# Attention stage of a two-block model kernel: projections by seven half-size products per 256 tokens, three weight slots, weight sums in the fourth slot, outputs kept in memory

## The reference, cut to what matters

```python
p  = h  @ w_in                      # 256 x 2048 times 2048 x (q | gate | z | k | v | xbc | dt)
pc = hc @ w_in[:, base:]            # the context tokens need k, v, xbc, dt of the first block
q, k, kc = rms_norm(heads(q)), rms_norm(heads(k)), rms_norm(heads(kc))
ya = neighbourhood_attention(q, k, v, kc, vc, rpb)      # softmax over 256 latent and 256 context keys
ya = ya * silu(gate)
yb = ...                                                # state space part, from z, xbc, dt
out = concatenate([ya, yb]) @ w_out
```

## Time and profile before

| | us |
|---|---|
| median of 3 runs | 2831.66 (2830.11 to 2832.17) |
| the profiled execution, its own time | 2830.7 |
| its span, first to last instruction | 2828.5 |
| TensorE busy in it | 2776.7 (98%) |
| VectorE busy | 1314.0 (46%) |
| ScalarE busy | 441.6 (16%) |
| GpSimd busy | 51.4 (2%) |
| mean granted TensorE clock | 0.992 of full |

### The profile page before, as it was taken

How to read it: one execution, slowest core, us unless ns; L and a number is a source line. 1 busy time by engine, 2 the same in 40 slices (tenths; PEclk the granted TensorE clock), 3 DMA queues, 4 the chain that set the end, 5 groups by cost and what they waited for, 6 DMA issues and landing times. The chain is left out here.

```text
span 2828.5 us, 38622 instructions
## 1 busy us (share of the span) xinstructions
PE 2776.7 (98%) x15840; PEld 2235.0 (79%) x15840; DVE 1314.0 (46%) x2317; ACT 441.6 (16%) x867; POOL 51.4 (2%) x72
## 2 busy tenths in 40 slices
PE   7999999999999999999999999999999999999999
PEld 1467866776686566666668888999999899999999
DVE  3643343333243245555555003665666665555543
ACT  0221111111111122222222001111111111121211
POOL 0010000000000000000000000000000000000000
PEclk9999999999999999999999999999999999999999
DMA  9874555655464133333332544555554545545542
GB/s 384 306 248 154 178 170 171 200 181 160 154 202 130 40 105 105 104 104 104 104 104 95 187 150 151 176 166 164 176 169 158 178 134 145 147 150 158 160 139 86
DMA packets 379174, 445.20 MB, mean 157 GB/s; under 512 B 20308, under 2 KB 351560, under 8 KB 378312
## 3 DMA queue, kind: packets, MB, share of 16 engines
q1 hardware_dynamic: 351088, 352.76, 40.6%
q0 software_dynamic: 19520, 75.50, 7.7%
q10 hardware_dynamic: 8472, 15.58, 1.5%
HBM read 439.56 MB, written 4.26 MB: 157 GB/s over the span
## 5 line engine op out<-in xcount | busy, mean ns | idle before, releaser
L529 PE MATMUL bank<-hT,w 128*128 128x128 f32 (+2 forms) x6128 | 1263.4, 365 | 6.1 <-ACT hT L1154 4.6
L529 PEld LDWEIGHTS bank<-hT,w 128*128 128x128 f32 x6128 | 898.2, 193 | 329.8 <-issue 296.1
L529 PE MATMUL bank<-w,hT 128*128 128x256 f32 (+2 forms) x2048 | 394.0, 353 | 0.0
L529 PEld LDWEIGHTS bank<-w,hT 128*128 128x128 f32 x2048 | 350.1, 190 | 48.9 <-issue 10.0
L1154 ACT ACTIVATE work<-bank 128x512 f32<-128x512 f32 (+3 forms) x282 | 146.1, 539 | 1300.3 <-PE bank L529 1295.1
L529 PE MATMUL bank<-yT,w 128*128 128x256 f32 (+1 forms) x1888 | 343.2, 342 | 1.4 <-DVE yT L1870 1.0
L529 PEld LDWEIGHTS bank<-yT,w 128*128 128x128 f32 x1888 | 307.3, 191 | 33.0 <-DVE yT L1870 1.2
L529 PE MATMUL bank<-hT,work 128*128 128x128 f32 x2352 | 279.5, 275 | 0.0
L529 PEld LDWEIGHTS bank<-hT,work 128*128 128x128 f32 x2352 | 270.9, 192 | 0.0
L1701 DVE SCALAR_TENSOR_TENSOR work<-xT,silc,work 128x512 f32<-128x512 f32 x240 | 180.5, 752 | 43.2 <-DMA xT<-in_ada_w 35.2
L1154 ACT ACTIVATE work<-work 128x512 f32<-128x512 f32 (+4 forms) x267 | 150.1, 562 | 245.2 <-DVE work L1767 149.4
(11 more groups left out here) (172 smaller groups left out, 1831.8 us busy)
## 6 DMA issues: line engine op xcount, KB each, us to landing
w<-in_na_ssd_w_in SPq DMA_DIRECT2D x48, 2048.0 KB, 8.4
xT<-in_ada_w POOLq DMA_DIRECT2D x64, 1024.0 KB, 5.6
w<-in_sc_w_in SPq DMA_DIRECT2D x32, 2048.0 KB, 10.3
w<-in_w_in SPq DMA_DIRECT2D x32, 2048.0 KB, 10.4
w<-in_na_ssd_w_out SPq DMA_DIRECT2D x16, 2048.0 KB, 8.4
w<-in_ada_w SPq DMA_DIRECT2D x12, 2048.0 KB, 11.2
w<-in_na_ssd_w_in SPq DMA_DIRECT2D x16, 1024.0 KB, 7.3
w<-in_sc_w_out SPq DMA_DIRECT2D x8, 2048.0 KB, 8.2
```

Source lines behind the costliest of these rows:

```text
L529: return nc.tensor.matmul(dst, lhsT, rhs, start=start, stop=stop, skip_group_check=free)
```

## The change

In `na` the tiles of all iterations are numbered n = 4i, 4i+1, ... (q, gate, k, v). A unit is one tile with 256 tokens: q, gate, k latent, k context, v latent, v context, six per iteration. The very first unit stays as it was; the other 47 are made by seven products of half size (7 x 8 matmuls of 128 columns, `na_unit`). Tiles go round three slots (n mod 3). The fourth slot now holds the weight sums (`turn`, four places of 8 x 128, three per tile in rotation); the fourth sum overwrites a quarter of the tile. VectorE makes them in two halves (`sums_one`, `sums_two`), one tile ahead. Sums of the latent tokens lie in the first half of `yT`, those of the context tokens in the second. So the attention outputs no longer fit there: `na_out` writes them to `yout`, ScalarE's queue stores them to memory after each pair of heads (`na_store`), and SyncE loads all of them back in the first `ssd` iteration. ScalarE copies the products to `staged0`, VectorE combines them (`na_combine`), and squares and the sigmoid start from the combined values. The loops of `na` are written out for all eight iterations. Norm and shift of the context tokens come after the first unit. The stage after changes only in its semaphore counts.

```diff
+    def na_places(n):
+        return [turn[:, (3 * n + m) % 4, :, :] for m in range(3)]
...
-        gp.wait_ge(norm_mul, 2 * DC)
+        gp.wait_ge(norm_mul, DC)
         iterations(gp, 8, late_chunks)
...
+                if phase == "ssd":
+                    return sp.wait_ge(acc_full, na_filled((30, 31, 29)[s]))
...
-        iterations(sp, 8, na)
+        for n in range(32):
+            if n < 3:
+                sp.wait_ge(ada_used, 10 + n)
+            else:
+                sp.wait_ge(acc_full, na_filled(n - 3))
+            at = (COL_Q, COL_GATE, COL_K, COL_V)[n % 4] + (n // 4) * TILE
+            load(na_slot(n), w_in[:, :, at:at + TILE])
+            if n % 4 == 1 and n > 4:
+                na_biases(n // 4 - 1)
...
                 sp.dma_start(xT[:, :, :].rearrange("p a b -> p (a b)"), x_scratch).then_inc(x_back, 16)
+                sp.wait_ge(y_saved, 16 * 8)
+                sp.dma_start(yT[:, 0:DC, :].rearrange("p a b -> p (a b)"), y_scratch).then_inc(y_back, 16)
...
+        def na_unit(i, u, midway=None):
...
+            wait(pe, acc_free, k - 1)
+            if n == 0:
+                featured(bank[0][:, 0:T], s, 0, T, lambda kc: kc + 1).then_inc(acc_full, 1)
+                featured(bank[1][:, 0:T], s, 1, T).then_inc(acc_full, 1)
+                return
...
+            product(a(0), quarter(s, 0, 0), x(0, 0), None, turned)
+            product(a(1), quarter(s, 1, 0), x(0, 1), None, turned)
...
+            pe.wait_ge(na_t, 3 * n - 2)
+            product(a(2), t1, sums[1], None, turned)
+            pe.wait_ge(na_t, 3 * n - 1)
+            product(a(3), t2, sums[2], None, turned).then_inc(acc_full, 1)
+            if midway:
+                midway()
+            pe.wait_ge(acc_free, k)
+            product(b(0), quarter(s, 0, 1), sums[3], None, turned)
+            product(b(1), quarter(s, 1, 1), sums[4], None, turned)
+            pe.wait_ge(na_t, 3 * n)
+            product(b(2), t4, x(1, 1), None, turned).then_inc(acc_full, 1)
...
+        def na_staging(i, u, part):
...
+            if part == 0:
+                wait(act, n_made, 6 * i + u)
+            width = 2 * P if i + u == 0 else (4 - part) * P
+            A(flat[:, 4 * P * part:4 * P * part + width], bank[part][:, 0:width], ACT.Copy).then_inc(acc_free, 1)
...
+        def na_store(a):
+            act.wait_ge(na_y, 2 * a + 2)
+            act.dma_start(y_scratch[:, 2 * a * T:(2 * a + 2) * T], yout.rearrange("p a b -> p (a b)")).then_inc(y_saved, 16)
...
+        def sums_one(n):
...
+            dve.wait_ge(w_loaded[s], 16 * (EARLY + n // 3 + 1))
+            if n > 1:
+                dve.wait_ge(acc_full, na_filled(n - 2))
+            link(v.tensor_tensor(places[0], quarter(s, 0, 1), quarter(s, 0, 0), ALU.subtract))
+            v.tensor_tensor(quarter(s, 0, 1), quarter(s, 1, 1), quarter(s, 0, 1), ALU.subtract).then_inc(na_t, 1)
+
+        def sums_two(n):
...
+            dve.wait_ge(acc_full, na_filled(n - 1, False))
+            v.tensor_tensor(places[1], quarter(s, 1, 1), places[0], ALU.subtract).then_inc(na_t, 1)
+            dve.wait_ge(na_t, 3 * n - 1)
+            v.tensor_tensor(places[2], quarter(s, 1, 0), places[1], ALU.subtract).then_inc(na_t, 1)
...
+        def na(i):
+            first = is_first(i)
             a = i - 1
-            if not is_first(i):
+            n = 4 * i
...
                 na_biases(a)
                 late_mod(a)
...
+                sums_one(n + 1)
+                late_part(i, 0)
+                sums_two(n + 1)
+                na_combine(i, 0, qraw)
+            sums_one(n + 2)
+            if not first:
                 na_softmax(a, 0, link)
+            sums_two(n + 2)
...
+            na_combine(i, 1, graw)
...
                 na_turned(a, 0)
                 na_softmax(a, 1, link)
...
+            sums_one(n + 3)
...
+            late_part(i, 1)
+            na_combine(i, 2, kraw[:, :, 0:T])
+            if not first:
                 na_out(a, 0)
                 na_turned(a, 1)
+            late_part(i, 2)
+            sums_two(n + 3)
+            late_part(i, 3)
+            na_combine(i, 3, kraw[:, :, T:T + TC])
+            if not first:
                 na_out(a, 1)
+            if i < 7:
+                sums_one(n + 4)
+            late_part(i, 4)
+            late_part(i, 5)
+            na_combine(i, 4, vtok[:, 0:2, :])
             dve.wait_ge(na_ge, i + 1)
...
+            late_part(i, 6)
+            late_part(i, 7)
+            if i < 7:
+                sums_two(n + 4)
...
+            na_combine(i, 5, vtok[:, 2:4, :])
```

More of the change, by code:

```diff
@@ L663, in na @@
             a = i - 1
[L664 to L668 removed]
+            na_unit(i, 0)
             if not first:
                 na_scores(a, 0)
[L671 to L675 removed]
+            na_unit(i, 1)
             if not first:
@@ L889, in _ @@
         norm_halves(1)
-        def product(dst, weights, tokens, ready=None, turned=False, chunks=range(EIGHT)):
-            for kc in chunks:
-                if ready:
-                    pe.wait_ge(ready[0], ready[1] + kc + 1)
-                a, b = weights[:, kc, :], tokens[:, kc, :]
-                last = mm(dst, b if turned else a, a if turned else b, kc == 0, kc == EIGHT - 1)
-            return last
         def banks_free(phase, s, i):
@@ L1208, in _, with shifted @@
         act.wait_ge(mod_ready, 1)
-        for k in range(2):
+        def shifted(k):
             for kc in range(DC):
@@ L1244, in na @@
             if not first:
                 na_exp(a, 0)
[L1246 to L1254 removed]
+            na_staging(i, 1, 0)
@@ L1255, in na @@
+            na_staging(i, 1, 1)
+            na_rms(i, 0)
             if not first:
                 na_exp(a, 1)
-            na_rms(i, 0)
+            for u in (2, 3):
+                na_staging(i, u, 0)
+                na_staging(i, u, 1)
             for ch in range(2):
-                full("na", 2 + ch, i)
-                A(kraw[:, ch, :], bank[ch][:, :], ACT.Copy)
-                A(ksq[:, ch, :], bank[ch][:, :], ACT.Square).then_inc(acc_free, 1)
-            for half in range(2):
-                na_rms(i, 1 + half)
-                full("na", 4 + half, i)
-                wait(act, na_po, 2 * i)
-                A(vtok[:, 2 * half:2 * half + 2, :].rearrange("p a b -> p (a b)"), bank[half][:, :],
-                  ACT.Copy).then_inc(acc_free, 1)
@@ L1269, in _ @@
-        iterations(act, 8, na)
+                na_square(i, 1 + ch, ksq[:, ch, :], kraw[:, ch, :], 3)
+            if not first:
+                na_store(a)
+            na_sigmoid(i)
+            na_staging(i, 4, 0)
+            na_staging(i, 4, 1)
+            na_rms(i, 1)
+            na_staging(i, 5, 0)
+            na_rms(i, 2)
+            na_staging(i, 5, 1)
+        for i in range(8):
+            na(i)
         for h in range(2):
             na_exp(7, h)
+        na_store(7)
         def ssd_setup():
@@ L1675, in na_out @@
             dve.wait_ge(na_po, 2 * a + h + 1)
-            v.tensor_tensor(chunk(yT, 2 * a + h), bank[5][:, 0:T], gsil[:, h, :], ALU.mult).then_inc(na_y, 1)
+            if h == 0:
+                wait(dve, y_saved, 16 * a)
+            v.tensor_tensor(yout[:, h, :], bank[5][:, 0:T], gsil[:, h, :], ALU.mult).then_inc(na_y, 1)
         def silu(out_, raw, sigmoid):
```

269 lines of the change are left out of this document (155 added, 114 removed).

## The result

The changed kernel takes **2819.2 us** (median of 7 runs, 2809.75 to 2821.61); the kernel before took 2830.67 on the same chip (median of 7, 2829.79 to 2835.14). The ratio is 0.995 with a 95% interval of 0.9936 to 0.9964: faster, but by 0.5% where 1.6% was forecast, and outside the range of 2770 to 2802. Every ratio in this document is to the kernel before, timed on the same chip as the kernel it is given for. The profiled execution took 2821.06 us, 37.3 more than the 2783.8 that the sum gave for it.

What follows compares the result with a forecast made beforehand. TensorE, busy 98% of the span, was taken to bound the kernel. 2830.7 - 60.9 (TensorE's work) + 12 (tail stall) + 2 (slower clock) = 2783.8; the median lies 1.0 higher, 2784.8 us, range 2770 to 2802.

Steps and rivals of the forecast that it cites:

- TensorE's work, 60.9 us: Attention stage: units of 12.507 us save 54.5 us in seven iterations and 6.4 in the first, if nothing makes TensorE wait.
- the first rival: Tail: the bias rows land before they are wanted, so no stall; 2770.8 us, chance 0.07.
- The last rival: Attention units: weight loads take turns with matmuls, 0.111 us more per record, 526 us slower, 3358 us; chance 0.01.
- VectorE's work: Attention iteration: weight sums add 19.6 us and combines 11.0, making 66.3 of 89.7 us; total and order fit.
- the schedule: One attention iteration, t = 0 at its first unit: VectorE's results dated against TensorE's needs, `late_sums` ending at 89.7 us.
- GpSimd's chunks: Attention loop: a chunk takes 5.5 us from issue until VectorE goes on; the closest is issued at 71, wanted at 80.
- the smallest reserve: End of an attention iteration: eighth late chunk taken at 83, `late_sums` at 88.0, 5 us to spare.
- small waits in every iteration: Rival, attention loop: late chunks cost 1 to 3 us in each of seven iterations; 2792 to 2806 us, chance 0.15.
- what would show the forecast wrong: Signs: period over 92 us, idle time before `late_sums` or a unit's third product, or a tail still 22 us.
- The tail: After the eighth attention iteration: late bias rows stall TensorE 12 us (9.3 to 18.4), slower clock adds 2 (0 to 4).
- From the first `ssd` product to the end: Everything after the attention tail: the same length as before the change.
- the bound: Rival, attention loop: VectorE limits it through late chunks; gain used up at 12 us late, 2848 us at 14; chance 0.04.

Runs made afterwards that it cites:

- Experiment 5: Changed kernel with the loop's bias rows issued behind the q load, the tail's issued earlier and masked before VectorE's last combine: 2770.6 us, ratio 0.9784.
- experiment 10: Changed kernel, bias transfers of iterations 1 to 6 replaced by aligned 256-byte rows 512 bytes apart, the same six for all partitions: 2796.81 us.
- experiment 7: Changed kernel, bias transfers of iterations 1 to 6 replaced by aligned 256-byte rows spread over a weight matrix: 2800.15 us; the profiled execution took 2812.06.
- experiment 6: Changed kernel, bias transfers of iterations 1 to 6 replaced by the same bytes in 1536-byte rows of a weight matrix: 2799.31 us.

## Why the prediction was wrong

**TensorE's work, 60.9 us: right.** A unit takes 12.5 us and the period, where nothing waits, is 89.77 us (89.7 forecast). Experiment 5 has neither loss, and its span is 2768.0 against 2828.5: 60.5 us less. The sum of the first rival, 2770.8 without a stalled tail, agrees with its 2770.6 to a microsecond. The rule cited from the Trainium skill, TensorE: Matmul & The Clock Gate, section The mechanism, by which, as the prediction reads it, loads and matmuls of whole arrays take turns, does not hold here. A record of 256 columns took 0.216 us in the kernel before (13.82 us for 64) and one of 128 columns 0.1117 (12.507 for 112), so only 0.007 us of a record does not grow with its columns. A load in turn would have to fit into that. The last rival's 0.111 us of load was busy time that runs beside the products.

**VectorE's work: right in size, wrong in the dates of the last chunks.** It is busy 66.46 us in the iteration from 411.9 to 501.8 (66.3 forecast), and its queue kept the dates of the schedule but for chunks seven and eight. **The step that failed** is "GpSimd's chunks: issue at 297.11, VectorE free to go on at 302.64, 5.5 us, and the closest one is issued at 71 and wanted at 80". The two dates came true: the seventh chunk of the second iteration was issued at t = 71 and wanted at 80, counted from 224.48. The landing did not: 16.9 us in place of 5.5. 5.5 us was read from one chunk that met no bias rows; in the same trace of the kernel before, between 200 and 890 us, chunks took 5.3 to 10.4 us. Even by 5.5 this chunk had 3.5 us to spare, not the 5 that the prediction calls the smallest reserve. In the new order the gate load goes out at t = 63 and the bias rows from 63 to 71, and the last three chunks at 63, 71 and 77: SyncE's loads were costed for their own dates only, and the bias rows of the loop were not in the schedule at all. The prediction named the effect as a rival, "small waits in every iteration" (2792 to 2806, chance 0.15), and priced it by idle time alone. Idle was 11.7 us, the slow clock behind it 13.8; with some 1.3 us of smaller pieces that makes 26.8 (22.7 in the periods, 4.1 in the first iteration, which took 85.48 us from its first product to `late_sums` against 81.39 in experiment 5). The period of over 92 us and the idle time before `late_sums` were both on the list of what would show the forecast wrong.

**The tail: right mechanism, size too small.** The stall is 18.69 us against 12, just outside the bounds of 9.3 and 18.4. From the v tile's last product at 873.00: the wait 0.2, the two loads 2.8 (2.3 forecast), the last bias issue 5.3 in (3.7), its landing 11.1 (6.4), the mask 0.96. The term that was mis-sized is the landing, taken from the median of the earlier trace rows, which also have one of 12.9: 4.7 of the 6.7 us. The issues add 1.6 and the loads 0.5. What differs from the kernel before is what comes right behind: 2 MB at 882.00 and 2 MB at 882.74, where SyncE issued nothing more for over 26 us then. The first three of the four bias transfers landed in 8.6, 6.3 and 7.0 us, and the last, issued just before those loads, in 11.1. That the loads make the last landing long was not tried. The sentence of the Trainium skill on DMA: Bandwidth & Descriptors, section Queues, rings and completion order, leaned to the upper half of the bounds. The trace agrees in that direction (18.69), without showing that ring order is the cause. The clock behind it cost 2.8 us (26.2 us of tail without the pause, 23.4 in experiment 5), 2 forecast. In the first 11.5 us behind the pause the granted clock was 0.65.

**From the first `ssd` product to the end**: 1901.0 us against 1898.2, where the same length was forecast. A wait of 0.68 us for `in_ssd_d` and 64 records that took 22.50 instead of 20.80 us make up most of it; the prediction had no term for either.

The whole: 26.8 in the loop, 7.3 in the tail, 2.8 behind it, 36.9 of the 37.3 us missed.

**The rivals that were wrong**: VectorE never became the bound. The one mechanism named there, a chunk that is late by over 5 us, was the right place, but the lateness that it needed (12 us) was not reached: VectorE's longest wait for a chunk was 8.2 us.

## What to carry to other kernels

When work moves to another time in a periodic schedule, list every transfer of every queue that is now in flight together, small ones too, and don't price a landing by a row in which the engines were free. Give a wait on TensorE's path its idle time and something for the slower clock behind it, 2 to 5 us in most cases here. And look at how a small transfer reads memory and what it stands behind: here 400 KB of overlapping rows per iteration, moved 30 us in time, were worth 26 us, and with the tail's moved too and the mask first the kernel reaches 2770.6 us, below the changed kernel's 2819.2 and the 2830.67 of the kernel before.

## What the runs showed of the hardware

- Behind pauses of 2.3 to 3.8 us TensorE's records ran slower for a while, at a cost of 3.45 us in each of the changed kernel's four; behind the first the granted clock was 0.53 for 5 us. That figure is no constant: behind the pauses before `late_sums` in the other traces (0.77 to 4.17 us) the same 48 records lost between 1.8 us (experiment 10, pause 2.87) and 4.6 us (experiment 7, pause 3.35), and the length of the pause doesn't order them. A short pause can cost more: in experiment 7 a wait of 0.67 us stood before 128 records that took 25.26 us, at a granted clock of 0.50 between 925 and 937 us, where experiment 6 has a wait of 0.48 and 14.51 us. That is most of the 12 us by which this execution is slower than the others of its kernel:

```profile
912.19 25.26 PE L560 MATMUL bank<-w,hT 128*128 128x64 f32 x128 [0.67 <-DMA work<-in_ssd_d]
...
911.67 14.51 PE L560 MATMUL bank<-w,hT 128*128 128x64 f32 x128 [0.48 <-DMA work<-in_ssd_d]
```

- Four transfers of 98 KB with 256-byte rows that start 31 elements apart in a partition and one element on for each partition, within about 1 KB, issued right behind a 2 MB load, bring the DMA rate down to 23 or 35 GB/s at the lowest, and 1 MB transfers of another queue take up to 15.3 and 16.9 us. The same number of 256-byte rows in the same place that are aligned and spread, odd and spread, or 512 bytes apart in one place leave these at 12.5 us or less (VectorE's waits 38 to 46 us against 61 and 70).
- Rows that lie back to back in memory and in a partition are moved as one: 144 packets under 512 bytes instead of 1680.
- How long SyncE takes to issue four small transfers depends on their rows and on what stands before them. Right behind a 2 MB load, four of 256-byte rows took 7.75 us and four of 1536-byte rows (the same bytes) 3.90; 3 us after such a load, the 256-byte ones took 3.00 (the kernel before) and 3.19 (experiment 1).
